# Hybrid GLA, pooling and gated DeltaNet layer on one core: decay sums moved into the projection stage, one decay matrix instead of two, merged forget-gate differences, keys moved by one place

## The chip, the cores and the metric

One core of a Trainium2 chip. The time is device microseconds (us) of one launch, which computes one layer for a prompt of 2048 tokens and a sample of 64 tokens.

## What is computed

Cut to what matters here:

```python
h = rmsnorm(x, norm_pre)
proj = h @ w_in                      # split: gla q,k,v,f,z; pool u,z; gdn q,k,v,a,b,z; three merge gates
# A: gated linear attention, chunked: logf = log_sigmoid(f @ wf2 + bf) / 16, b = cumsum(logf)
att = sum_d q[i,d] * k[j,d] * exp(b[i,d] - b[j,d])           # j <= i
# C: gated DeltaNet, chunked WY form: g = -exp(a_log) * softplus(a + dt_bias), beta = sigmoid(b)
G = cumsum(g)                                                # within a chunk
dec = exp(where(j <= i, G[i] - G[j], -inf))
m = beta[i] * (k @ k.T) * dec (j < i);   a_qk = (q @ k.T) * dec
u_bar, w = solve(I + m, [beta * v, beta * exp(G) * k])
q_dec = q * exp(G);   k_dec = k * exp(G_last - G);   state = exp(G_last) * state + k_dec.T @ u
# then head norms, SiLU gates, three branch projections, sigmoid merge gates, w_out, norm, residual
```

The kernel works in chunks of 128 tokens (16 for the prompt, numbered 0 to 15) and one of 64 (chunk 16, the sample).

## The kernel before

The program has five stages, each a block in which all engines run their own list of instructions and meet only at semaphores: the norm of x (norm_phase), the projections (project_phase), the chunks (chunk_phase), the branch projections and the output. All large products are made of three matmuls on operands split into a high and a low part (hi*hi, hi*lo, lo*hi).

**Projection stage.** TensorE multiplies one block of 128 columns of w_in after another (L411 to L413) with all 2112 tokens, in six tiles of 352. Each block's weights are split by GpSimd (L171, L173). The first block, F_SPECIAL, holds the rows from which decay g and beta come. VectorE works on these rows in a chain in which each link waits for the one before (L688 to L700): it ends with `X = X * nega * -1`, the decays g, on 4 partitions and 2112 tokens. Only then does VectorE take the tiles of the forget gates out of PSUM (L709), which TensorE makes in forget_gates (L428), waiting on side_free. SP stores the rows into scratch_feat, a DRAM tensor with 31 rows per partition and token; row R_GB has g and beta.

**Chunk stage.** Per chunk all engines work on the same chunk, and TensorE's list holds, between the chunk's own small matmuls, 48 steps of gate_products: a step is three matmuls 352 wide (L1255) of the merge-gate projection, whose last 16 blocks of columns were left for this stage. A tile of 352 tokens takes 8 steps, a chunk has 6 tiles. The steps stand in the list by hand, as filler where TensorE would wait. ScalarE copies each tile out (gates_out, L1456) when all its 8 steps are done and the row buffer is stored. The weights of a pair of chunks' gates, gate_w, are loaded by SP (L1129) and split by GpSimd into gate_w_hi and gate_w_lo (L1518, L1520), one block in the middle of a chunk and one at its end.

A wait is written now(engine, name, chunk) for something of this chunk and before(engine, name, chunk) for something that the previous chunk must have let go. The order of a chunk:

- SP loads the chunk's 31 rows (`inputs`, L1124, two buffers), two chunks ahead, after the stores of the outputs. Its sem_inc of h_good (L1171), after the first loads, lets the first gate product go.
- TensorE turns the row of g and beta (gbt, L1265), the values (vt, L1268) and the keys (kt, L1272). VectorE copies decay_beta (L1637). TensorE sums g down the chunk by a matmul with a triangle: as a column (g_col, L1277) and, with g broadcast as weights, as a row on all partitions (grow, L1282). ScalarE copies g_row (L1465) and makes e_row = exp(g_row) (L1469).
- GpSimd makes dec_qk = g_row - g_col and, with two additive masks, the arguments of two decay matrices (L1542 to L1549); ScalarE takes both exponentials (dec_kk L1474, dec_qk L1476). GpSimd makes k_dec (L1553), and q_dec (L1562) later.
- VectorE scans the forget gates (b_sum, L1633) and makes F: b_sum and 8 differences for each of two halves of 128 elements, 18 instructions (L1643 to L1652). ScalarE makes F its absolute value and then its exponential (L1480, L1483), with gates_out(c, 1) between them. VectorE multiplies keys by F (KF, L1691), GpSimd queries by F (QF, L1559).
- VectorE: d_col (L1659), k_tok (L1662), M from KK and dec_kk (L1667), M0, X, att from QK and dec_qk (L1679), XT, U (L1686), then KF.
- A triangular inverse in six more levels: for each level TensorE makes Z (L1370), turns XT (L1376), multiplies (L1385), and VectorE masks Z (L1704), copies X (L1708) and updates XT (L1717). The pairs of the linear attention (L1330) and the own pairs of level 1 (L1340) stand between them.
- U, outputs, state updates and head norms end the chunk.

## Time and profile before

| | us |
|---|---|
| median of 3 runs | 2978.51 (2978.11 to 2989.63) |
| span of the profiled execution | 2980.0 |
| TensorE matmul busy | 2742.3 (92%) |
| VectorE busy | 1141.0 (38%) |
| GpSimd busy | 840.4 (28%) |
| ScalarE busy | 664.2 (22%) |
| chunk stage, first to last gate product | 1211.1 to 2353.4 |
| mean granted TensorE clock, share of 2.4 GHz | 0.934 |

The profiled execution's own time is given only as its span. Busy times count an instruction from its start to its end, so one that waits for a resource counts as busy too, and a matmul's end is modelled and overlaps the next one's start. A span of an instruction group in the timeline runs from the first start to the last end.

### The profile page before, as it was taken

What the parts mean: (1) busy time and instruction counts of PE and PEld (TensorE: products, weight loads), DVE (VectorE), ACT (ScalarE), POOL (GpSimd) and SP (SyncE); (2) the same over time, 40 slices, a digit from 0 to 9 for tenths busy, and PEclk for the clock granted to TensorE, in tenths of its full rate; (3) what the DMA queues carried; (4) which work ended last, traced back from release to release, by engine and by line L of the source; (5) the groups of instructions that cost most, each with busy time, mean ns of one, the idle gap of its engine ahead of it and who ended that gap; (6) DMA issues with size and microseconds to landing.
All of it is one profiled execution on the core that took longest, in us unless ns stands there. A gap on an engine that the chain in (4) does not pass through costs nothing. (4 is left out here: it accounts for less than half of the span.)

```text
span 2980.0 us, 42847 instructions
## 1 busy us (share of the span) xinstructions
PE 2742.3 (92%) x17449; PEld 2602.6 (87%) x17449; DVE 1141.0 (38%) x1708; ACT 664.2 (22%) x997; POOL 840.4 (28%) x598
## 2 busy tenths in 40 slices
PE   6999999999999899799999989889999869999898
PEld 5899999999888899688888888888888759999786
DVE  5310112144656400444445444544545443331333
ACT  6121111112544111121221222112222132220221
POOL 1112111111111111344333444434444213442122
PEclk9999999999999999899999989989999769997799
DMA  4022411011111221322222243222221335542343
GB/s 159 23 108 94 174 65 58 29 51 57 44 65 66 72 74 44 114 64 64 64 67 64 64 141 110 79 77 74 71 67 38 114 123 169 170 157 76 114 144 107
DMA packets 208221, 261.80 MB, mean 88 GB/s; under 512 B 20864, under 2 KB 183056, under 8 KB 202320
## 3 DMA queue, kind: packets, MB, share of 16 engines
q1 hardware_dynamic: 201840, 251.01, 25.7%
q0 software_dynamic: 6240, 8.65, 1.0%
q8 instruction: 120, 1.97, 0.3%
q14 instruction: 21, 0.17, 0.0%
HBM read 160.34 MB, written 99.29 MB: 87 GB/s over the span
## 5 line engine op out<-in xcount | busy, mean ns | idle before, releaser
L411 PE MATMUL dense<-h_hi_first,w_hi 128*128 128x352 f32 x1080 | 356.0, 330 | 15.5 <-ACT row_y L658 8.5
L171 POOL TENSOR_TENSOR w_hi<-w_raw,zero 128x1024 fp32r<-128x1024 f32 x45 | 86.3, 1917 | 953.6 <-PE dense L413 916.0
L412 PE MATMUL dense<-h_lo_first,w_hi 128*128 128x352 f32 x1080 | 353.4, 327 | 0.0
L413 PE MATMUL dense<-h_hi_first,w_lo 128*128 128x352 f32 x1080 | 353.0, 327 | 0.0
L411 PE MATMUL dense<-h_hi_second,w_hi 128*128 128x352 f32 x1080 | 348.1, 322 | 0.0
L413 PE MATMUL dense<-h_hi_second,w_lo 128*128 128x352 f32 x1080 | 347.0, 321 | 0.0
L412 PE MATMUL dense<-h_lo_second,w_hi 128*128 128x352 f32 x1080 | 346.7, 321 | 0.0
L1255 PE MATMUL gate_bank<-h_hi_first,gate_w_hi 128*128 128x352 f32 x768 | 296.7, 386 | 33.0 <-SPq L1171 16.0
L1921 PE MATMUL y<-o_hi,wo_hi 128*128 128x256 f32 (+1 forms) x864 | 254.6, 295 | 26.3 <-DVE o_lo L1956 26.3
L1255 PE MATMUL gate_bank<-h_lo_first,gate_w_hi 128*128 128x352 f32 x768 | 260.5, 339 | 0.0
L1255 PE MATMUL gate_bank<-h_hi_first,gate_w_lo 128*128 128x352 f32 x768 | 259.2, 337 | 0.0
L1923 PE MATMUL y<-o_lo,wo_hi 128*128 128x256 f32 (+1 forms) x864 | 254.5, 295 | 0.0
L1925 PE MATMUL y<-o_hi,wo_lo 128*128 128x256 f32 (+1 forms) x864 | 254.5, 295 | 0.0
L411 PEld LDWEIGHTS dense<-h_hi_first,w_hi 128*128 128x128 f32 x1080 | 207.1, 192 | 19.3 <-ACT row_y L658 8.7
L412 PEld LDWEIGHTS dense<-h_lo_first,w_hi 128*128 128x128 f32 x1080 | 206.9, 192 | 1.1
L413 PEld LDWEIGHTS dense<-h_hi_first,w_lo 128*128 128x128 f32 x1080 | 206.9, 192 | 0.0
L413 PEld LDWEIGHTS dense<-h_hi_second,w_lo 128*128 128x128 f32 x1080 | 203.2, 188 | 0.0
L412 PEld LDWEIGHTS dense<-h_lo_second,w_hi 128*128 128x128 f32 x1080 | 202.9, 188 | 0.0
L411 PEld LDWEIGHTS dense<-h_hi_second,w_hi 128*128 128x128 f32 x1080 | 202.6, 188 | 0.0
L1921 PEld LDWEIGHTS y<-o_hi,wo_hi 128*128 128x128 f32 x864 | 177.8, 206 | 27.0 <-DVE o_lo L1956 27.0
L1255 PEld LDWEIGHTS gate_bank<-h_hi_first,gate_w_hi 128*128 128x128 f32 x768 | 157.3, 205 | 49.2 <-SPq L1171 16.3
L1577 POOL TENSOR_TENSOR gla_att<-gla_att,masked 128x256 f32<-128x256 f32 (+1 forms) x118 | 85.2, 722 | 334.2 <-DVE masked L1697 326.3
(227 smaller groups left out, 5288.3 us busy)
## 6 DMA issues: line engine op xcount, KB each, us to landing
inputs<-scratch_feat SPq DMA_DIRECT2D x16, 1984.0 KB, 8.9
scratch_feat<-row_y SPq DMA_DIRECT2D x28, 1056.0 KB, 4.9
gate<-scratch_gates SPq DMA_DIRECT2D x16, 1536.0 KB, 7.2
w_raw<-in_w_in SPq DMA_DIRECT2D x45, 512.0 KB, 5.4
scratch_gates<-gate_row SPq DMA_DIRECT2D x96, 176.0 KB, 1.8
gate_w<-in_w_in SPq DMA_DIRECT2D x32, 512.0 KB, 5.2
o_raw<-scratch_branch_out SPq DMA_DIRECT2D x8, 1536.0 KB, 10.4
scratch_gates<-row_y SPq DMA_DIRECT2D x8, 1056.0 KB, 5.0
```

The costliest lines, as they stand in the source:

```text
L171: nc.gpsimd.tensor_tensor(self.hi[:, p], raw, zeros, ALU.add).then_inc(self.high_ready, 1)
L411: nc.tensor.matmul(out, w_hi[:, p, k], h_hi[:, k, cols], start=(k == 0), stop=False)
L412: nc.tensor.matmul(out, w_hi[:, p, k], h_lo[:, k, cols], start=False, stop=False)
L413: mm = nc.tensor.matmul(out, w_lo[:, p, k], h_hi[:, k, cols], start=False, stop=(k == KD - 1))
L1255: mm = matmul(gate_bank[:, T % 2, 0:TW], w[:, r, k], h[:, k, t * TW:(t + 1) * TW], start=(k == 0 and part == 0), stop=(k == KD - 1 and par ...
L1577: ins = tt(own, own, halves_packed(masked[0:n, :, l, 0:n // 2], s), ALU.add)
L1921: nc.tensor.matmul(out, wo_hi[:, k, cols], o_hi[:, p, k, 0:n], start=(k == 4 * b), stop=False)
L1923: nc.tensor.matmul(out, wo_hi[:, k, cols], o_lo[:, p, k, 0:n], start=False, stop=False)
L1925: mm = nc.tensor.matmul(out, wo_lo[:, k, cols], o_hi[:, p, k, 0:n], start=False, stop=(k == 4 * b + 3))
```

## The change

Seven edits; all but the first are in the chunk stage.

1. In the projection stage VectorE writes the decays to T and then makes their sums within each chunk with 17 scans, 16 of 128 elements and one of 64, so that row R_GB of scratch_feat holds G instead of g.
2. SP loads, behind every load of inputs, the four rows of G onto all 128 partitions with one broadcasting DMA into g_row, which gets two buffers. The matmuls g_col and grow, their copies and the buffer g_col go. decay_beta now holds the column of G.
3. There is one decay matrix: ScalarE makes dec = |G_j - G_i| with four instructions, one per head, with the column as bias, and dec = exp(-dec). VectorE's M uses it as it is; GpSimd multiplies it by the triangle into att, and VectorE multiplies att by QK in place. GpSimd's three decay instructions go.
4. The scans of the forget gates write F directly, and each difference is one instruction for both halves.
5. keys() (the two KF instructions) moves from behind U to behind the diagonal of level 1, which is behind the first Z.
6. ScalarE instead of GpSimd makes gate_w_hi. TensorE's filler steps are spread anew, kt stands before vt, vtg before KK.
7. On TensorE, ScalarE and VectorE the last two chunks of the prompt stand outside the loop.

```diff
@@ project_phase, vector
-                link(nc.vector.tensor_scalar(X[g_rows, 0, 0:NT], X[g_rows, 0, 0:NT],
+                link(nc.vector.tensor_scalar(T[g_rows, 0:NT], X[g_rows, 0, 0:NT],
                                              small[g_rows, S_NEGA:S_NEGA + 1], -1.0, ALU.mult, ALU.mult))
+                for c in range(CHUNKS + 1):
+                    at = slice(c * P, c * P + (P if c < CHUNKS else NS_))
+                    last = nc.vector.tensor_tensor_scan(X[g_rows, 0, at], ones[g_rows, 0:at.stop - at.start],
+                                                        T[g_rows, at], 0.0, ALU.mult, ALU.add)
+                link(last)
@@ chunk_phase
+    FILL = {"start": 2, "turned": 5, "KK": 3, "QK": 7, "m0t": 3, "first": 4, "z": 3, "level": 2, "last": 2}
@@ sync, load
                     sp.dma_start(inputs[:, p, :, 0:n], feat[:, :, bass.ds(c * P, n)]).then_inc(in_landed[p], 16)
+                    g = feat[AT_G:AT_G + HEADS, R_GB, bass.ds(c * P, n)]
+                    sp.dma_start(g_row[:, p, :, 0:n], g.rearrange("(a h) t -> a h t", a=1)
+                                 .to_broadcast([P, HEADS, n])).then_inc(row_landed[p], 16)
@@ tensor, chunk
-                    gate_products(2)
+                    gate_products(FILL["start"])
...
                     transpose(ring[0][0:n, 0], I[:, R_GB, 0:n], ident).then_inc(S["gbt"], 1)
+                    before(pe, "dSg_taken", c)
+                    for h in range(HEADS):
+                        mm = transpose(ring[2][0:n, h], I[:, R_GDN_K + h, 0:n], ident)
+                    mm.then_inc(S["kt"], 1)
                     before(pe, "SSQg_taken", c)
                     for h in range(HEADS):
                         mm = transpose(ring[1][0:n, h], I[:, R_GDN_V + h, 0:n], ident)
                     mm.then_inc(S["vt"], 1)
...
-                    gate_products(2)
-                    now(pe, "gb_taken", c)
-                    matmul(ring[0][0:n, 1, 0:HEADS], upper[0:n, 0:n], decay_beta[0:n, 0, :],
-                           start=True, stop=True).then_inc(S["gcol"], 1)
-                    gate_products(5)
-                    now(pe, "gcol_taken", c)
-                    for h in range(HEADS):
-                        mm = matmul(ring[0][:, h, 0:n], decay_beta[0:n, 0, h:h + 1].to_broadcast([n, P]),
-                                    upper[0:n, 0:n], start=True, stop=True)
-                    mm.then_inc(S["grow"], 1)
+                    gate_products(FILL["turned"])
+                    now(pe, "gb_taken", c)
+                    for h in range(HEADS):
+                        mm = transpose(ring[0][0:n, h], I[:, R_GLA_V + h, 0:n], ident)
+                    mm.then_inc(S["vtg"], 1)
                     now(pe, "vt_taken", c)
                     for h in range(HEADS):
                         k = I[:, R_GDN_K + h, 0:n]
                         mm = matmul(ring[1][0:n, h, 0:n], k, k, start=True, stop=True)
                     mm.then_inc(S["KK"], 1)
-                    gate_products(5)
+                    gate_products(FILL["KK"])
                     now(pe, "kt_taken", c)
...
                     mm.then_inc(S["QK"], 1)
-                    gate_products(2)
-                    now(pe, "grow_taken", c)
-                    for h in range(HEADS):
-                        mm = transpose(ring[0][0:n, h], I[:, R_GLA_V + h, 0:n], ident)
-                    mm.then_inc(S["vtg"], 1)
-                    gate_products(6)
+                    gate_products(FILL["QK"])
...
                     mm.then_inc(S["m0t"], 1)
-                    gate_products(1)
+                    gate_products(FILL["m0t"])
...
-                        gate_products(3 if l == 1 else 2)
+                        gate_products(FILL["first"] if l == 1 else FILL["level"])
...
-                        gate_products({1: 1, LEVELS - 1: 2}.get(l, 0))
+                        gate_products({1: FILL["z"], LEVELS - 1: FILL["last"]}.get(l, 0))
@@ scalar, chunk
+                    act.wait_ge(row_landed[p], i * 16 + 16)
+                    activation(e_row[:, :, 0:n], g_row[:, p, :, 0:n], ACT.Exp).then_inc(S["e_row_ready"], 1)
+                    now(act, "gb_taken", c)
+                    for h in range(HEADS):
+                        last = activation(dec[0:n, h, 0:n], g_row[0:n, p, h, 0:n], ACT.Abs,
+                                          bias=decay_beta[0:n, 0, h:h + 1], scale=-1.0)
+                    last.then_inc(S["dec_diff"], 1)
+                    now(act, "dec_diff", c)
+                    activation(dec[0:n, :, 0:n], dec[0:n, :, 0:n], ACT.Exp, scale=-1.0).then_inc(S["dec_ready"], 1)
                     now(act, "vt", c)
                     copy(v_tok[0:n], ring[1][0:n]).then_inc(S["vt_taken"], 1)
-                    copy(g_row[:, :, 0:n], ring[0][:, :, 0:n]).then_inc(S["grow_taken"], 1)
...
-                    activation(dec_kk[0:n, :, 0:n], dec_kk[0:n, :, 0:n], ACT.Exp, scale=-1.0) \
-                        .then_inc(S["dec_kk_ready"], 1)
-                    activation(dec_qk[0:n, :, 0:n], dec_qk[0:n, :, 0:n], ACT.Exp) \
-                        .then_inc(S["dec_qk_ready"], 1)
...
                     gates_out(c, 2)
+                    split_gate_w(c, 0)
                     gates_out(c, 3)
...
                     head_norm(c, n, 1, "SSQg", "SSQg_taken", "rsg_ready")
+                    split_gate_w(c, 1)
+
+                def gate_w_to_high(c, r):
+                    act.wait_ge(gate_w_landed[r], c * 16 + 16)
+                    copy(gate_w_hi[:, r], gate_w[:, r]).then_inc(gate_w_high, 1)
+
+                def split_gate_w(c, r):
+                    if not (isinstance(c, int) and c >= CHUNKS - 1):
+                        gate_w_to_high(c + 1, r)
@@ gpsimd, chunk
-                    tt(dec_qk[0:n, :, 0:n], g_row[0:n, :, 0:n],
-                       g_col[0:n].rearrange("p (a b) -> p a b", b=1).to_broadcast([n, HEADS, n]),
-                       ALU.subtract).then_inc(S["diff_ready"], 1)
-                    now(pool, "diff_ready", c)
-                    before(pool, "KK_taken", c)
-                    tt(dec_kk[0:n, :, 0:n], dec_qk[0:n, :, 0:n], over_heads(masks[0:n, M_POS:M_POS + n]), ALU.add)
-                    tt(dec_qk[0:n, :, 0:n], dec_qk[0:n, :, 0:n], over_heads(masks[0:n, M_NEG:M_NEG + n]),
-                       ALU.add).then_inc(S["dec_args"], 1)
...
+                    now(pool, "dec_ready", c)
+                    tt(att[0:n, :, 0:n], dec[0:n, :, 0:n], over_heads(upper[0:n, 0:n]),
+                       ALU.mult).then_inc(S["dec_qk_ready"], 1)
@@ vector, chunk
                     for b in range(2):
-                        last = nc.vector.tensor_tensor_scan(b_sum[:, b, 0:n], ones[:, 0:n], I[:, R_LOGF + b, 0:n],
+                        last = nc.vector.tensor_tensor_scan(F[:, 0, b, 0:n], ones[:, 0:n], I[:, R_LOGF + b, 0:n],
                                                             0.0, ALU.mult, ALU.add)
...
+                    tt(d_col[0:n], g_row[0:n, p, :, n - 1], decay_beta[0:n, 0], ALU.subtract) \
+                        .then_inc(S["dcol_diff"], 1)
+                    bs = F[:, 0, :, 0:n]
+                    for l in range(LEVELS):
+                        blocks = bs.rearrange("p b (m t) -> p b m t", t=2 * s)
+                        tt(F[:, l + 1, :, 0:n].rearrange("p b (m t) -> p b m t", t=2 * s), blocks,
+                           blocks[:, :, :, s - 1:s].to_broadcast([P, 2, n // (2 * s), 2 * s]), ALU.subtract)
...
                             tt(gla_att[0:n, :, 0:n], ring[0][0:n, :, 0:n], over_heads(ident[0:n, 0:n]),
                                ALU.mult).then_inc(S["diag_taken"], 1)
+                            keys()
```

The other filler counts (3, 1, 1, 2, 2 at the end of a chunk) stay.

## Rows read from the trace of the kernel before

**Rows 1.** The head of the page.

```profile
span 2980.0 us, 42847 instructions
```

**Rows 2.** What TensorE waited for: line, releaser; us in total, times, longest.

```profile
PE ring L1282 <- DVE g_col L1655: 58.0, 16, 4.3
PE level_bank L1385 <- DVE Z L1704: 31.3, 16, 2.5
...
PE gate_bank L1255 <- SPq L1171: 16.0, 1, 16.0
...
PE ring L1315 <- DMA gla_state<-in_state_gla: 2.4, 1, 2.4
```

**Rows 3.** Stretches; after the engines' busy times: granted clock, DMA share, GB/s.

```profile
1291.40:1298.30 6.90, 5.96 (x25) 5.96 (x26) 1.74 (x8) 1.66 (x4) 3.11 (x3) 0.51 0.93 294
1311.90:1318.80 6.90, 5.99 (x26) 5.89 (x26) 2.30 (x5) 0.00 (x0) 4.64 (x2) 0.51 0.01 2
2078.20:2085.00 6.80, 3.52 (x27) 3.48 (x27) 3.99 (x19) 1.66 (x4) 1.63 (x3) 1.00 1.05 336
```

**Rows 4.** Timeline of TensorE in chunk 1: start, us, line, [idle before].

```profile
1283.29 0.27 PE L1265 MATMUL ring<-constants,inputs 128*128 128x128 f32 x1
...
1285.24 0.28 PE L1277 MATMUL ring<-decay_beta,masks 128*128 128x4 f32 x2
1285.38 0.41 PE L1255 MATMUL gate_bank<-h_hi_first,gate_w_hi 128*128 128x352 f32 x1
...
1287.71 0.32 PE L1255 MATMUL gate_bank<-h_hi_first,gate_w_lo 128*128 128x352 f32 x1
1292.34 2.07 PE L1282 MATMUL ring<-masks,decay_beta 128*128 128x128 f32 x8 [4.31 <-DVE g_col L1655]
...
1299.46 1.05 PE L1293 MATMUL ring<-inputs 128*128 128x128 f32 x8
...
1307.91 1.00 PE L1370 MATMUL level_bank<-XT,M 128*128 128x64 f32 x8
...
1310.24 0.43 PE L1255 MATMUL gate_bank<-h_hi_first,gate_w_hi 128*128 128x352 f32 x1
```

**Rows 5.** Timeline of VectorE in the same chunk.

```profile
1283.82 6.45 DVE L1650 TENSOR_TENSOR F<-b_sum 128x128 f32<-128x128 f32 x7
...
1290.52 1.49 DVE L1650 TENSOR_TENSOR F<-b_sum 128x128 f32<-128x128 f32 x7
...
1296.18 0.69 DVE L1662 TENSOR_TENSOR k_tok<-ring,d_col 128x512 f32<-128x512 f32 x1 [0.94 <-ACT d_col L1472]
...
1307.27 5.15 DVE L1691 TENSOR_TENSOR KF<-inputs,F 128x1024 f32<-128x1024 f32 x2
```

**Rows 6.** Timelines of ScalarE and GpSimd in the same chunk.

```profile
1283.24 0.63 ACT L1447 ACTIVATE sq_gla<-sq_gla 128x512 f32<-128x512 f32 x1
...
1283.94 1.30 POOL L1590 TENSOR_TENSOR out_gla<-out_gla,sq_gla 128x512 f32<-128x512 f32 x1 [0.54 <-ACT sq_gla L1447]
...
1287.23 2.48 POOL L1520 TENSOR_TENSOR gate_w_lo<-gate_w,gate_w_hi 128x1024 fp32r<-128x1024 f32 x1
...
1309.09 2.26 POOL L1562 TENSOR_TENSOR q_dec<-inputs,e_row 128x512 f32<-128x512 f32 x1
```

**Rows 7.** Groups by line, 1205 to 2365 us: busy us, mean ns | idle before.

```profile
L1480 ACT ACTIVATE F<-F 128x2304 f32<-128x2304 f32 (+1 forms) x17 | 35.0, 2057 | 0.0
...
L1469 ACT ACTIVATE e_row<-g_row 128x512 f32<-128x512 f32 (+1 forms) x17 | 10.5, 617 | 0.5
...
L1633 DVE TENSOR_TENSOR_SCAN b_sum<-constants,inputs 128x128 f32<-128x128 f32 (+1 forms) x34 | 12.3, 404 | 12.0 <-DMA inputs<-scratch_feat 11.5
```

**Rows 8.** Timeline of SP's DMA issues as the chunk stage begins.

```profile
1211.64 5.82 SPq L1129 DMA_DIRECT2D gate_w<-in_w_in  x1
```

**Rows 9.** Timelines of VectorE and GpSimd in the projection stage.

```profile
117.69 1.10 DVE L709 TENSOR_SCALAR row_t<-side,small 128x352 f32<-128x352 f32 x2 [4.71 <-PE side L428]
...
116.87 1.89 POOL L171 TENSOR_TENSOR w_hi<-w_raw,zero 128x1024 fp32r<-128x1024 f32 x1 [25.75 <-PE dense L413]
```

More of the change, by code:

```diff
@@ L1089, in chunk_phase @@
         in_landed = [held.add(nc.alloc_semaphore(f"in_landed{p}")) for p in range(2)]
+        row_landed = [held.add(nc.alloc_semaphore(f"row_landed{p}")) for p in range(2)]
         masks_landed = held.add(nc.alloc_semaphore("masks_landed"))
@@ L1506, in _ @@
                 preload(act, ACT_)
+                for r in range(2):
+                    gate_w_to_high(0, r)
                 act.sem_inc(gate_taken, 2)
@@ L1686, in chunk, with keys @@
                     tt(U[0:n], v_tok[0:n], ring[2][0:n], ALU.subtract).then_inc(S["R_taken"], 1)
[L1687 to L1692 removed]
+                    def keys():
+                        now(dve, "F_ready", c)
+                        before(dve, "kdtg", c)
+                        for b in range(2):
+                            k = I[:, R_GLA_K + b:R_GLA_K + b + 1, 0:n].to_broadcast([P, LEVELS + 1, n])
+                            last = tt(KF[:, :, b, 0:n], k, F[:, 1:LEVELS + 2, b, 0:n], ALU.mult)
+                        last.then_inc(S["KF_ready"], 1)
                     def take_pairs(h):
```

95 lines of the change are left out of this document (30 added, 65 removed).

## The prediction

> **What bounds the kernel now.** The first thing to read is the span [rows 1] and which stage the diff touches: the chunk stage, from 1211 to about 2408 us, plus a short piece of the projection stage. In the chunk stage TensorE is the engine that sets the pace, so the second view is the list of what TensorE waited for [rows 2]. Two waits stand out in it: before the decay-row matmuls of L1282, for VectorE's g_col (58.0 us over 16 chunks, 3.6 each), and before the first product of the levels, L1385, for VectorE's Z (31.3 us, 1.96 each).
>
> The third view is the table of stretches with the granted clock [rows 3]. Right after each of the two waits the clock stands at 0.51 for 6.9 us, which is the 1.2 GHz level; 2.4 GHz is 1.00. A stretch of 6.9 us at half the clock costs about 3.4 us, so the two waits cost nearly as much again in clock as in idle time. The last row is the exception: in one chunk the g_col wait of 3.28 us was followed by 2.4 GHz. I take from this that gaps of 2 to 4 us usually, but not always, cost a fall.
>
> The fourth view is the timeline of one chunk, engine by engine, in the order of the rows. For TensorE [rows 4] the gate products fill the gaps: 15 matmuls start between 1285.38 and 1287.71, 0.166 us apart, so a step of three is 0.5 us. For VectorE [rows 5] the same seven F differences take 6.45 us the first time and 1.49 us the second (0.21 each). GpSimd's rows [rows 6] say why: out_gla, gate_w_hi and gate_w_lo run from 1283.94 to 1289.7, exactly under the slow seven. VectorE gets about one difference through for each GpSimd instruction. The same is seen at the keys: the KF pair takes 5.15 us while q_dec, in between, takes 2.26 us instead of the 1.3 us of out_gla with as many elements; the extra 1.0 us is one KF. So a KF alone is about 1.05 us, and the two engines take strict turns when VectorE reads both operands from SBUF. k_tok, with one operand in PSUM, takes 0.69 us beside GpSimd's work and is not held.
>
> The Trainium skill says this more sharply (SBUF — State Buffer, Who interferes with whom): the port pair is an exclusive lock held for the whole instruction. By that rule moving keys() does not make it cheap; it only changes which GpSimd instruction it meets, and the trace agrees with the turns above.
>
> **The change, part by part.** I count from the start of the gbt transpose of a chunk (1283.29 in rows 4), in us.
>
> *Removed matmuls.* The eight row matmuls (L1282, rows 4) are 2.07 us busy at 1.2 GHz, so 1.0 at 2.4; the g_col product stands 0.14 us ahead of the next gate product (1285.24 to 1285.38), and one break in the gate products less saves about 0.1. That is 1.2 us per chunk. The 3.6 us wait for g_col goes too.
>
> *The new front.* Eight matmuls 128 wide, like QK's of 1299.46, are 1.05 us busy with their tail and keep TensorE 0.8 us from its next work; four turns take half of that. TensorE: gbt, kt, vt 0.9, five steps 2.5, four turns of gla_v 0.4: it stands before KK at 3.8 and needs v_tok. ScalarE is free at 0.6 (the last Exp of the previous chunk, rows 6) and must now do in order: the high half of gate_w, 1024 elements; e_row; four Abs; the Exp of dec; v_tok. From 512 elements in 0.617 us and 2304 in 2.06 [rows 7] an element costs 0.8 ns and a start 0.2 us: 1.0 + 0.6 + 4 x 0.3 + 0.6 + 0.6 = 4.0, done at 4.6. **New wait 1: 0.75 us** before KK. Its bounds are 0 (all instructions overlapping) and 1.3 (each Abs 0.14 dearer for its per-partition bias, which no row shows alone).
>
> By the Trainium skill (ScalarE: Activation LUTs, What ACT_TABLE_LOAD costs) an activation with a per-partition bias pointer takes 280 ns + 0.833 ns per element and neighbours overlap by 93 ns. An estimate from that page is 0.29 us for each Abs, so the sum would be the same to 0.1 us.
>
> *k_tok.* KK ends at 5.4, three steps bring TensorE to 6.9, where QK waits for k_tok. VectorE's 16 differences and two copies become eight differences of 256 elements, about 0.35 us each alone (0.21 for 128, 0.69 for 512, rows 5). GpSimd is busy under them: out_gla until 1.95, gate_w_lo 2.4 (rows 6; its high half has left for ScalarE, and three decay instructions are gone), k_dec 1.3, the new mask product 1.3, ending at 7.2 with VectorE's turns. Four differences go through in these turns, the other four after them: 8.7; k_tok 0.7: 9.4. **New wait 2: 2.5 us.** Bounds: 0 (if VectorE were not held, 8 x 0.35 would be done by 3.6) and 3.9 (one more turn behind a 1.3 us instruction). I take 2.5 because the seven slow differences of rows 5 follow the turns to 0.2 us.
>
> *The middle.* QK until 10.2, seven steps and m0t 3.9, three steps 1.5, R 0.8, four steps 2.0: Z of level 1 starts at 18.4. Z and the own pairs are 2.33 (1307.91 to 1310.24): 20.7. VectorE does gla_att (0.65) and only then the keys, at 21.4. Z's mask is no longer behind them, so the 1.96 us wait before L1385 goes. But L1717's update of XT, which level 2 waits for, is now behind the keys. TensorE has three steps, the products and two steps, 3.4 us, and is at level 2 at 24.1.
> GpSimd meanwhile: ScalarE's F Exp waits behind gates_out(1), whose tile is complete 16 steps into the chunk, at 13.2; 0.4 + 2.1 gives F_ready at 15.7; QF, twice gate_w_lo's 1024 elements, 4.7, q_dec 1.3: 21.7; then gate_w_lo, whose high half is ready. So KF runs 21.7 to 22.8, gate_w_lo takes its turn to 25.2, the second KF is done at 26.3, the update at 26.7. **New wait 3: 2.6 us** before level 2. Bounds: 0.1 (no turn lost) and 3.9 (q_dec and gate_w_lo both before a KF).
>
> *Sum per chunk.* Off: 1.2 + 3.6 + 1.96 = 6.8. On: 0.75 + 2.5 + 2.6 = 5.85. Net 1.0 us less, 16 us in 16 chunks.
>
> *Clock.* Wait 3 is longer than the Z wait it replaces and is followed by short matmuls, so I keep its low stretch in every chunk. Wait 2 is shorter than g_col's usual 3.4 to 4.3; with the exception of rows 3 in mind I let the clock fall in two chunks of three. Saved: 5.3 x 3.4 = 18 us. The ends are 0 and 54.
>
> *Once.* (a) SP now issues a row load behind each inputs load, before it raises h_good, on which TensorE's first gate product waits (L1171 in rows 2). The issue that follows an inputs load took 5.82 us [rows 8]. The second row load will take that place: +6 us, bounds 1 and 8. In the loop the same block falls where SP blocks on gate_w now, some 10 us ahead of the first ScalarE instruction that needs that gate_w: nothing there, and if this cover went, gates_out(3), U and the head norms would queue on ScalarE behind that wait. The rows have a whole chunk to land. (b) The 17 scans on VectorE. The first side tile was taken at 117.69, after 4.71 us of idle, so the chain ended at 112.98 [rows 9]. A scan of 128 elements is 0.40 us busy [rows 7], about 0.34 with its overlap, so the chain is 5.8 us longer, and GpSimd's weight split at 116.87 holds the last ones, so the side tile is taken near 122.7: +5 us (bounds 1, and 8.5 with a clock fall). (c) The sample chunk gains nothing: its R waits for the state to land (2.4 us in rows 2). *At nothing:* att now first holds the masked decay, with the same two engines and waits as before it; peeling the last two chunks leaves their work unchanged, covered by TensorE's queued gate products; without that cover, a few us.
>
> **Total.** -16 - 18 + 11 = -23 us on a span of 2980.0. The page gives only the span, which stands 1.5 above the median of 2978.51. Forecast 2956.
>
> **The rivals.** A measurement here can tell 0.5%, 15 us, from no change.
> 1. *The clock falls at both new waits in all chunks*, as it did at the g_col gap of rows 3. Then -16 + 11 = -5: 2974, no change. For: the gaps before L1385, 2.0 us on average, were followed by one too. Chance 0.25.
> 2. *Level 2 becomes the bound (slower).* If both KF instructions meet a GpSimd instruction that has not begun when they ask (q_dec, then gate_w_lo), wait 3 is 3.9 and the low clock that follows covers Z, x_turned, pairs and the next level, 1.7 us more per chunk. With rival 1's clock that is -5 + 16 x (1.3 + 1.7) = +43; with wait 3 grown alone about +16. It decides from 2.2 us over my per-chunk sum. For: q_dec and the keys come within 0.3 us of each other. Against: the first KF asked while q_dec ran, in my schedule. Time 2995 to 3021, chance 0.17.
> 3. *The differences miss GpSimd*, because ScalarE hands over gate_w's high half later than out_gla ends, or k_dec waits for e_row. Then wait 2 is under 1 us and the clock stays up there: 1.7 + 2.3 more per chunk, -23 - 64: 2891. Chance 0.10.
> 4. *The keys miss gate_w_lo.* Wait 3 is 0.2, and its low stretch goes: -23 - 16 x 5.8: 2863. Against: the high half is ready 2 us before q_dec ends. Chance 0.08.
> My forecast, 2920 to 2963, has 0.40. That the change does not do what it says I rule out: nothing issues the removed matmuls any more.
>
> **The numbers.** Faster by over 0.5%: 0.40 + 0.10 + 0.08 = 0.58; within: 0.25; slower: 0.17. The likeliest case alone spans 2920 to 2963; the range that leaves out 2 in 10 is 2880 to 2995.
>
> **What would show it.** In the profile after, TensorE's waits should list KK behind ScalarE's v_tok (about 12 us), QK behind VectorE's k_tok (about 40), and L1370 behind XT's update (about 42); g_col and Z must be gone. One or two low stretches per chunk, on average 1.7. The difference instructions should show some over 1.5 us and others at 0.35; gate_w_lo should have every second one near 3.4 us. The forecast is wrong if k_tok's wait is under 1 us, or if level 2 has none, or if TensorE's first gate product is not late by about 6 us.

## The result and the profile after

The changed kernel takes 3008.9 us (median of 17 runs, 2989.6 to 3023.9) against 2981.6 for the kernel before (17 runs on the same chip). The ratio is 1.0085, with a 95% interval of 1.0067 to 1.0103: slower by 0.85%. The forecast was 2956, faster. One execution of a later kernel, the one with the early start, ran at a mean clock of 0.553 and took 4415 us; it is left out of that kernel's ratio, and its median without it is 2854.55.

The profiled execution spans 3022.2 us, 42.2 more than [rows 1]; it is the slowest of the 17, and the medians lie 27 us apart. This is the page's head and its table of busy times:

```profile
span 3022.2 us, 42253 instructions
PE 2773.5 (92%) x17279; PEld 2629.2 (87%) x17279; DVE 1123.5 (37%) x1538; ACT 697.2 (23%) x1063; POOL 737.4 (24%) x531
```

TensorE issues 170 matmuls fewer and is busy 31 us longer, which points at the clock. The mean granted clock fell from 0.934 to 0.916. As the clock has two levels here, 1.00 and 0.50, the time at the low one is 2 x (1 - mean) x span: 393 us before, 508 after. I use this sum for the profiled execution of every run below and call it the low time. It varies within one kernel, and the time goes with it: over the 17 runs of the changed kernel it runs from 430 us, in the one of 2989.6, to 508, in the one of 3023.9, with 469 at the median. That is about 0.44 us of time for each microsecond more at the low level.

What TensorE waited for in the chunk stage (us in total, times, longest), to be read against [rows 2]:

```profile
PE level_bank L1350 <- DVE XT L1692: 39.3, 20, 2.4
PE ring L1278 <- DVE k_tok L1635: 34.2, 16, 2.6
PE gate_bank L1245 <- SPq L1159: 25.7, 1, 25.7
PE gate_bank L1245 <- SPq L1176: 13.3, 1, 13.3
...
PE ring L1295 <- DMA gla_state<-in_state_gla: 7.5, 1, 7.5
...
PE ring L1273 <- ACT v_tok L1455: 3.5, 5, 1.8
```

L1350 is Z's product of level 2 and up, L1278 is QK, L1273 KK, L1245 the gate products, L1295 R. The waits for g_col and Z, 89.3 us together, are gone. The three new ones are where they were forecast, 77.0 us together. The one before level 2 is 2.43 us in 15 of the 16 chunks; the last has no gate_w left to split. So the waits inside the chunks fell by 12 us, and yet the kernel is slower.

Where the time is lost shows in one chunk of the second half. This is TensorE's timeline of chunk 12, only the rows with an idle time ahead and the products of the levels:

```profile
2116.27 1.25 PE L1278 MATMUL ring<-inputs 128*128 128x128 f32 x8 [2.11 <-DVE k_tok L1635]
...
2135.20 1.97 PE L1350 MATMUL level_bank<-XT,M 128*128 128x64 f32 x8 [2.43 <-DVE XT L1692]
...
2144.76 1.80 PE L1350 MATMUL level_bank<-XT,M 128*128 128x64 f32 x8
...
2154.15 1.29 PE L1350 MATMUL level_bank<-XT,M 128*128 128x64 f32 x8
2159.48 1.00 PE L1350 MATMUL level_bank<-XT,M 128*128 128x64 f32 x8
2164.51 1.00 PE L1350 MATMUL level_bank<-XT,M 128*128 128x64 f32 x8
```

From level 4 to 5 and from 5 to 6 it is 5.33 and 5.03 us, but from level 2 to 3 and from 3 to 4 it is 9.56 and 9.39. The table of stretches (start and end; length, the engines' busy times, then the granted clock, DMA share, GB/s) gives the reason:

```profile
2117.20:2120.60 3.40, 3.40 (x15) 3.40 (x14) 2.03 (x4) 0.57 (x1) 0.00 (x0) 0.50 1.00 236
2120.60:2134.20 13.60, 12.11 (x83) 11.42 (x81) 6.67 (x6) 4.35 (x5) 9.26 (x4) 1.00 0.31 108
2134.20:2154.60 20.40, 19.40 (x83) 18.51 (x84) 5.26 (x10) 0.45 (x1) 0.00 (x0) 0.50 0.00 1
2154.60:2180.00 25.40, 25.21 (x193) 23.96 (x193) 11.35 (x24) 3.47 (x7) 5.13 (x7) 1.00 0.04 15
```

After the wait for k_tok the clock is at the 1.2 GHz level for 3.4 us, half of what it was after the g_col wait [rows 3]. In this chunk it then falls 1.0 us before the wait ahead of level 2 ends, and stays low for 20.4 us, three times the 6.9 of [rows 3]; 19.4 of them count as busy. Chunks 9 to 14 all look like this one.

The first half is mixed. Chunk 5 has the same wait of 2.43 us and the same work behind it, but the clock falls 1.6 us after the wait has ended, and comes back after 6.8 us:

```profile
1613.94 1.11 PE L1350 MATMUL level_bank<-XT,M 128*128 128x64 f32 x8 [2.43 <-DVE XT L1692]
```

```profile
1615.60:1622.40 6.80, 6.80 (x30) 6.68 (x31) 1.67 (x3) 0.00 (x0) 0.00 (x0) 0.51 0.01 2
```

Over the 15 chunks with this wait the stretch is 6.8 us in four, 10.2 in one, 17 in two, 20.4 in seven and 27.2 in one, 16 on average. In the seven with 20.4 the clock fell 0.8 to 1.0 us before the wait ended. After the wait for k_tok there is a stretch of 3.4 us in 11 chunks and none in the other five.

The instructions that make TensorE wait are as forecast. VectorE's and GpSimd's timelines of chunk 12, first at its head, then at the keys:

```profile
2108.41 2.35 DVE L1619 TENSOR_TENSOR d_col<-g_row,decay_beta 128x4 f32<-128x4 f32 x1
2110.68 4.60 DVE L1629 TENSOR_TENSOR F<-F 128x256 f32<-128x256 f32 x7
...
2129.93 4.88 DVE L1665 TENSOR_TENSOR KF<-inputs,F 128x1024 f32<-128x1024 f32 x2
2134.73 0.41 DVE L1692 TENSOR_TENSOR XT<-XT,level_bank 128x256 f32<-128x256 f32 x1
```

```profile
2108.35 2.39 POOL L1511 TENSOR_TENSOR gate_w_lo<-gate_w,gate_w_hi 128x1024 fp32r<-128x1024 f32 x1
2110.70 1.53 POOL L1532 TENSOR_TENSOR k_dec<-inputs,e_row 128x512 f32<-128x512 f32 x1
...
2129.13 1.28 POOL L1544 TENSOR_TENSOR q_dec<-inputs,e_row 128x512 f32<-128x512 f32 x1
2130.37 3.35 POOL L1511 TENSOR_TENSOR gate_w_lo<-gate_w,gate_w_hi 128x1024 fp32r<-128x1024 f32 x1
```

Even a d_col of four elements takes 2.35 us, until the gate_w_lo that began 0.06 us earlier lets it through. At the keys the first KF waits for the end of q_dec, gate_w_lo comes in between, and the second KF is done at 2134.7.

The start of the stage, SP's DMA issues, against [rows 8]:

```profile
1207.44 0.34 SPq L1152 DMA_DIRECT2D masks<-in_masks  x1
...
1208.99 7.63 SPq L1111 DMA_DIRECT2D g_row<-scratch_feat  x1
...
1218.11 9.11 SPq L1111 DMA_DIRECT2D g_row<-scratch_feat  x1
```

The first gate product starts at 1227.32 instead of 1211.12. The masks' load was issued at 1201.00 before and at 1207.44 now, so 6.4 us come from the projection stage and 9.8 from SP's queue.

My theory after this view: the wait before level 2 lets the clock fall, and it does not come back while TensorE does the thin work of the first levels (few gate products between small matmuls that wait for one another); all the rest of the change gains. The rivals were that the new spread of the gate steps starves the levels whatever VectorE does, and that the loss lies in the projection stage and the start.

### The profile page after: what moved, and what is told of

The parts are those of the page before. It is cut to its first block and busy times, and to the rows that moved or that the text cites. A ratio compares the mean times of both kernels' runs of the same rounds, so it can differ in the third digit from the quotient of the medians.

```text
span 3022.2 us, 42253 instructions
## 1 busy us (share of the span) xinstructions
PE 2773.5 (92%) x17279; PEld 2629.2 (87%) x17279; DVE 1123.5 (37%) x1538; ACT 697.2 (23%) x1063; POOL 737.4 (24%) x531
## 5 line engine op out<-in xcount | busy, mean ns | idle before, releaser
L1245 PE MATMUL gate_bank<-h_hi_first,gate_w_hi 128*128 128x352 f32 x768 | 297.4, 387 | 47.5 <-SPq L1159 25.7
L1245 PE MATMUL gate_bank<-h_lo_first,gate_w_hi 128*128 128x352 f32 x768 | 264.1, 344 | 0.0
L1245 PE MATMUL gate_bank<-h_hi_first,gate_w_lo 128*128 128x352 f32 x768 | 263.6, 343 | 0.0
L392 PEld LDWEIGHTS dense<-h_hi_first,w_hi 128*128 128x128 f32 x1080 | 206.6, 191 | 19.5 <-ACT row_y L639 8.7
L1245 PEld LDWEIGHTS gate_bank<-h_hi_first,gate_w_hi 128*128 128x128 f32 x768 | 159.1, 207 | 63.5 <-SPq L1159 26.0
```

The lines of the kernel that those rows point to most:

```text
L392: nc.tensor.matmul(out, w_hi[:, p, k], h_hi[:, k, cols], start=(k == 0), stop=False)
L1245: mm = matmul(gate_bank[:, T % 2, 0:TW], w[:, r, k], h[:, k, t * TW:(t + 1) * TW], start=(k == 0 and part == 0), stop=(k == KD - 1 and par ...
```

## The experiments

Twelve kernels ran, three or five rounds each. "Before" is 2982 to 2983 us in all of them.

### Keys put back

The keys() call goes from behind the diagonal back to behind U; everything else of the change stays.

```diff
+                    keys()
...
-                            keys()
```

> The changed kernel with one part undone: keys() stands behind U again, so VectorE's update of XT is no longer behind the keys, and the mask of Z is. Theory 1 (the wait of TensorE before level 2, and the low clock that then lasts through the levels, is what made the change slow): the wait before the Z product of level 2 (39.3 us in the changed kernel) is gone, a wait before the xt product of level 1 comes instead, about 0.9 us per chunk, 15 in all (1.96 before, less two more gate steps); the stretches of 20 us at the low clock are gone, so that the low time is near the 397 us of the kernel before instead of 508. Time: 3009 - 24 for the waits - about 50 for the clock, near 2935. Theory 2 (the new spread of the gate steps leaves the levels with too little work, whatever VectorE does): the long low stretches stay, and only the 24 us of waits go: near 2985. Theory 3 (the cost lies in the projection stage and in the first row load alone): no more than the wait's difference either, 2985.

Measured: 2889.95 us, ratio 0.9687 (0.9671 to 0.9702). What TensorE waited for in this kernel:

```profile
PE ring L1278 <- DVE k_tok L1635: 34.4, 16, 2.7
...
PE level_bank L1365 <- DVE Z L1679: 11.4, 16, 0.7
```

The wait before level 2 is gone, the 0.7 us wait before level 1's product came as expected, and no long stretch follows it; the stretch from before level 1's product through the levels of a chunk is at full clock:

```profile
2031.80:2060.00 28.20, 27.48 (x215) 26.24 (x214) 13.27 (x24) 0.82 (x2) 9.85 (x10) 1.00 0.02 7
```

The mean clock is 0.953, the low time 272 us instead of 508. One edit of seven accounts for 119 us; the other six together make the kernel before 93 us faster. The two rivals, which gave 2985, are out. My own theory gave 2935, because it left the low time at 397 us, that of the kernel before. There the g_col wait and the Z wait were each followed by 6.8 us in most chunks; here only the k_tok wait is followed by a low stretch, 3.4 us in 10 of the 16 chunks. That is as in the changed kernel (11), so what went is the stretch at the levels.

### GpSimd's gate_w_lo behind the keys, then behind the differences too

```diff
+                        now(pool, "KF_ready", c)
                         split_gate_w(c + 1, 0)
```

> The changed kernel with one wait added: GpSimd does not begin gate_w_lo of the middle of the chunk before VectorE has finished the keys. Nothing else differs. Theory 1: the keys take about 1.1 us each instead of 1.1 and 3.4 to 4.9, XT comes in time, the wait before level 2 falls from 2.4 to at most 0.3 us per chunk, and with it the long low stretch: -35 us of waits and 50 to 90 us of clock, 2885 to 2925. Theory 2 (the spread of the gate steps): -35 us only, about 2975, with the long low stretches still there. Rival 3 (the low clock comes from the wait before QK, whatever follows): the low stretch behind QK stays and now runs through to the levels, 2975 too.

Measured: 2877.25 us, ratio 0.9650 (0.9634 to 0.9665), just below the range given. The keys stay where the change put them. The wait for k_tok is unchanged (34.7 us in 16) and the long stretches at the levels are gone all the same, so the rival that put them down to it is out. Only GpSimd waits, and TensorE's wait before level 2 is 0.25 us in this chunk:

```profile
2020.90 1.11 PE L1350 MATMUL level_bank<-XT,M 128*128 128x64 f32 x8 [0.25 <-DVE XT L1693]
```

```diff
+                    if swap:
+                        load_h(2)
                     if not (isinstance(c, int) and c >= CHUNKS - 1):
+                        now(pool, "F_diffs", c + 1)
                         split_gate_w(c + 1, 1)
-                    if swap:
-                        load_h(2)
```

> As the run before it, and GpSimd's gate_w_lo at the start of a chunk also waits, until VectorE's eight differences of that chunk are done. So VectorE has no GpSimd instruction beside its differences but out_gla. Expected by the account of turns: the differences take about 0.35 us each but for two, k_tok is ready 2 us earlier, and the wait before QK (34.2 us in the changed kernel) falls to under 10; with it the low stretch of 3.4 to 6.8 us behind it in most chunks: 25 us of waits and about 25 of clock less than the run before, 2840 to 2880. If VectorE's differences are slow for another reason than GpSimd's SBUF traffic, the wait before QK stays at 2 us and the time is that of the run before. What it may cost: k_dec now stands behind gate_w_lo that starts later, so the outputs and state updates of the chunk could wait for k_dec; by the schedule it has 40 us to spare.

Measured: 2860.25 us, ratio 0.9596 (0.9568 to 0.9624), in the range. The wait for k_tok fell from 34.2 to 7.7 us in total, 0.5 at most, and k_dec's delay cost nothing that TensorE's waits show. The median came down by 17 us where 25 us of waits and some clock had been promised: the wait at the change of halves (L1176) had grown to 19.7 us. That is taken up below.

### The kernel before with its keys moved

The same move alone, in the kernel before.

> The kernel before with that one part of the change alone: keys() moved to behind the diagonal of level 1. The Z wait (31.3 us) goes, and a wait before the Z product of level 2 comes. TensorE has only one gate step behind Z here where the changed kernel has three, and GpSimd does both halves of gate_w there, so the new wait is about 1 us longer than in the changed kernel, 3.5 us per chunk, 56 us. Theory 1: it is followed by the long low stretch through the levels; 2981 - 31 + 56 + 20 to 60 for the clock: 3025 to 3065. Theory 2 (it was the spread of gate steps): the stretch of 6.8 us behind the wait stays as it was, near 3005. If moving the keys is harmless here, 2981 or below.

Measured: 3040.93 us, ratio 1.0199 (1.0177 to 1.0222), in the range of theory 1.

```profile
PE ring L1282 <- DVE g_col L1655: 57.9, 16, 4.3
PE level_bank L1370 <- DVE XT L1719: 54.1, 20, 4.7
```

The Z wait of [rows 2] (31.3 us) went, 54.1 us came, and the mean clock fell to 0.923, 468 us of low time. The move is harmful by itself, without anything else of the change (58 us here, 119 in the changed kernel).

### Gate steps moved around the wait

First, two steps go from ahead of the wait to behind level 2's first products.

```diff
-    FILL = {..., "z": 3, "level": 2, "last": 2}
+    FILL = {..., "z": 1, "level": 2, "last": 2, "behind": 2}
...
+                        if l == 2:
+                            gate_products(FILL["behind"])
```

> The changed kernel with two gate steps of the middle of each chunk (1 us) moved from ahead of the wait before level 2 to behind its products, ahead of the pairs. The idle time there grows from 2.4 to about 3.4 us per chunk, and the work that follows it is denser. Theory 1a (the long low stretch comes from the idle time alone): it stays 20 us in as many chunks or comes in more of them, and the time rises by 16 us for the waits and up to 30 for the clock, to 3025 to 3055. Theory 1b (it comes from idle time followed by the thin matmuls of the levels): the clock falls as often, but comes back earlier, low stretches of 7 to 10 us instead of 20, 3009 + 16 - 40 to 60, 2965 to 2985.

Measured: 2990.88 us, ratio 1.0032 (1.0018 to 1.0046). The wait rose to 54.2 us in 20, as meant, and the low time fell from 508 to about 413 us (mean clock 0.931; over all runs the median went from 469 to 412). The kernel was 18 us faster with 15 us more of waiting. Neither theory had the number, but the direction is that of 1b: with two more gate steps behind the wait the stretches were 6.8 to 13.7 us long and 3.4 once, never 17 to 27. The longest, in chunk 1, with the clock falling 1.2 us before the wait's end:

```profile
1322.40:1336.20 13.80, 12.54 (x53) 12.04 (x53) 3.37 (x6) 0.00 (x0) 0.00 (x0) 0.51 0.00 1
```

The fair comparison is between chunks in which the clock falls at the same point of the wait, 0.8 to 1.2 us before its end. With the levels at once behind it the stretch is 20.4 to 20.6 us in all 17 such chunks (seven of the changed kernel, five with one step moved, two with two keys more, three of the kernel before with its keys moved). With two gate steps behind it, it is 13.6 to 13.8 us in all four. At the Z wait of the kernel before, where the fall came 0.6 to 1.7 us before the end, it is 6.8 to 7.0 in all 14. So the work behind the wait does set the stretch once the moment of the fall is the same. Where the clock falls after the wait's end, the stretch before the levels is 6.8 to 17 us, and 27.2 once; what decides there, and what sets the moment of the fall, no run here shows.

Then two steps, and in a later run one, go from ahead of the first Z to behind it.

```diff
-    FILL = {..., "first": 4, "z": 3, ...}
+    FILL = {..., "first": 2, "z": 5, ...}
```

> The changed kernel with two gate steps moved from ahead of the first Z to behind it, still ahead of the wait before level 2, so that this wait falls from 2.4 to about 1.4 us if the keys end when they did (they are asked for 1 us earlier, but GpSimd's turns fix their end). Nothing is taken away from GpSimd or VectorE. If the fall of the clock hangs on the length of the wait, the long low stretches go in most chunks: -16 us for the waits and -50 to -90 for the clock, 2900 to 2945. If any wait at this place makes it fall, they stay, and the time is about 2993.

> The changed kernel with one gate step, not two, moved from ahead of the first Z to behind it: the keys are asked for 0.5 us earlier instead of 1.0. By the account of turns q_dec has then still begun 0.3 us before the keys ask, so the first key instruction waits for q_dec's end as it did, the second for gate_w_lo, both end when they did, and the wait before level 2 stays 2.4 us: 3009, no change. If the time went with the moment of asking in a smooth way, it would be half way between 3009 and 2877, 2943.

Measured: 2877.46 us for two steps, ratio 0.9656 (0.9633 to 0.9678); 3013.76 for one, 1.0093 (1.0069 to 1.0117). One step of 0.5 us changes nothing, two give 131 us. VectorE's and GpSimd's timelines of chunk 1 with two steps:

```profile
1312.83 3.52 DVE L1665 TENSOR_TENSOR KF<-inputs,F 128x1024 f32<-128x1024 f32 x2
1316.27 0.41 DVE L1692 TENSOR_TENSOR XT<-XT,level_bank 128x256 f32<-128x256 f32 x1
```

```profile
1312.98 2.28 POOL L1544 TENSOR_TENSOR q_dec<-inputs,e_row 128x512 f32<-128x512 f32 x1
1315.22 3.34 POOL L1511 TENSOR_TENSOR gate_w_lo<-gate_w,gate_w_hi 128x1024 fp32r<-128x1024 f32 x1
```

In the first of the two runs my expectation was wrong in its mechanism: I expected the keys to end when they did, and a wait of 1.4 us. But the keys now ask 0.15 us before q_dec begins. So the first KF runs ahead of q_dec (which is held and takes 2.28 us), the second ahead of gate_w_lo, the pair takes 3.52 instead of 4.88 us, and TensorE has no wait at level 2 at all (2.6 us in 4 places are left of 39.3 in 20). For one step I then worked by the turns, and that held: q_dec has still begun first, and the wait is 38.9 us in 20, against 39.3. The moment of asking counts only by which side of a GpSimd instruction's start it falls on. The Trainium skill's rule of the exclusive lock (SBUF — State Buffer, Who interferes with whom) agrees with these rows.

### A wait of chosen length at level 2

In the kernel where gate_w_lo waits for the keys, VectorE does its second key instruction twice, or three times (`m` is 1 or 2), so that TensorE waits though GpSimd has no part in it.

```diff
+                        for j in range(m):
+                            last.then_inc(again, 1)
+                            dve.wait_ge(again, c * m + (j + 1))
+                            last = tt(KF[:, :, 1, 0:n], k, F[:, 1:LEVELS + 2, 1, 0:n], ALU.mult)
                         last.then_inc(S["KF_ready"], 1)
```

> The kernel in which gate_w_lo waits for the keys (2877 us, no wait before level 2), with VectorE's second key instruction done twice, one behind the other: nothing meets it on GpSimd, so the update of XT comes about 1.1 us later and TensorE waits about 1 us before level 2. This is a wait of chosen length at the place in question, with the turns taken out of it. If the clock's fall depends on the length of the wait, 1 us is short enough (0.7 us before the products of level 1 brought none when the keys were put back): +16 us for the waits alone, 2893. If any wait there makes the clock fall through the levels, + 16 + 16 x up to 8 for the clock, 2950 or more.

> The same with the second key instruction done three times: XT comes about 2.2 us later, a wait of 2.1 to 2.4 us before level 2 as in the changed kernel, though GpSimd has no part in it. If idle time there and the thin work behind it are the whole cause of the long low stretch, the low time of the chunks comes back to near the 399 us of the changed kernel and the time to 2877 + 35 + 70 to 100: 2980 to 3010. If GpSimd's and VectorE's contention matters for TensorE's clock in some other way, only the waits come: 2912.

Measured: 2967.23 us for one, ratio 0.9943 (0.9924 to 0.9963); 3019.73 for two, 1.0151 (1.0117 to 1.0184). Against 2877 that is 90 and 142 us, of which the waits are 21 and 41 (27.4 and 48.3 us against 6.8). The second is 10 us above the range given. TensorE in one chunk of the run with one more, and its stretches:

```profile
2026.50 1.10 PE L1351 MATMUL level_bank<-XT,M 128*128 128x64 f32 x8 [1.50 <-DVE XT L1698]
2034.05 1.80 PE L1351 MATMUL level_bank<-XT,M 128*128 128x64 f32 x8
2043.44 1.80 PE L1351 MATMUL level_bank<-XT,M 128*128 128x64 f32 x8
```

```profile
2028.40:2045.40 17.00, 17.00 (x77) 16.43 (x76) 3.70 (x8) 0.45 (x1) 0.23 (x1) 0.51 0.03 12
```

And in the run with two more:

```profile
2055.10:2075.50 20.40, 18.98 (x81) 18.08 (x82) 5.70 (x10) 0.45 (x1) 2.35 (x1) 0.51 0.00 1
```

The second run shows what was in question: idle time at this place, with the thin work behind it, costs the clock without GpSimd. The low time is 458 us (477 at the median of its four runs, against 469), the kernel 11 us slower than the changed one with a wait of 2.76 instead of 2.43 us. In the first run I was wrong. I had thought that about a microsecond would do no harm, as 0.7 us before level 1's product does none; the wait came out at 1.5 us, and the clock fell behind it in all 16 chunks, 0.3 to 3.3 us after its end. Its low time is 416 us.

The chunks shown are the longest cases. With one more key the stretch is 6.8 us in ten chunks, 10.2 in three, 13.6 in two and 17 in the one above, where the fall comes 2.3 us after the wait's end. With two more it is 6.8 in seven, 10.2 in four, 17 in three and 20.4 in two.

Nor is a long wait needed. The three kernels with both waits of gate_w_lo idle 0.25 us before level 2, and in four of their 48 chunks the clock fell all the same, about 3 us later, for 13.6 us in which TensorE was busy throughout. This is one of them, from the first of the three:

```profile
2119.00:2132.60 13.60, 13.60 (x60) 13.08 (x60) 3.21 (x6) 0.45 (x1) 0.00 (x0) 0.51 0.00 1
```

### SP's queue

The three raises of h_good go ahead of both row loads at the start, and then, in one more kernel, ahead of chunk 9's loads at the change of halves. Both have the two waits of gate_w_lo.

```diff
-                load(0, 0)
+                load(0, 0, row=False)
                 load_gate_w(0, 1, 0)
-                load(1, 1)
-
                 for t in range(3):
                     sp.sem_inc(h_good[t], CHUNKS // 2)
+                load_row(0, 0)
+                load(1, 1)
```

> The kernel with both waits of gate_w_lo (2860 us), and with SP's three raises of h_good at the start of the stage ahead of both row loads, with the first inputs and the gate weights before them. TensorE's first gate product then waits for the gate weights and their split alone: the wait of 25.7 us becomes 10 or less, and the low stretch of 27 us behind it may shrink. If the row loads cost what I now put down to them (7.7 and 9.0 us of issue on SP, of which 9.7 delay the start) and the rest of the wait is SP's other issues, 2860 - 10 to 20: 2840 to 2850. If the start is bound by the landing of the gate weights, no more than 5 us come.

> The kernel with the early start and both waits of gate_w_lo (2855 us), and at the change of halves SP raises h_good ahead of chunk 9's loads of inputs and row instead of behind them. In that kernel the row load's issue there took 15 us and TensorE waited 19.5 us, with 20 us at the low clock behind it. If the row load on SP's queue is the cause, that wait falls to under 5 us: -15 for it and about -8 for the clock, 2830. If the landing of the second half of h is the cause, nothing changes: 2855.

Measured: 2854.88 us, ratio 0.9570 (0.9552 to 0.9588), and 2832.56, ratio 0.9512 (0.9486 to 0.9538). The first can hardly be told from the 2860 without it: the wait at the start fell from 25.7 only to 20.3 us. SP's issues show a part of the reason:

```profile
1211.01 0.64 SPq L1109 DMA_DIRECT2D inputs<-scratch_feat  x1
1211.70 7.56 SPq L1121 DMA_DIRECT2D gate_w<-in_w_in  x1
```

Now the gate weights' load stands behind the inputs load and takes the 7.6 us that the row load took. It is the place behind an inputs load that costs, not the row load as such. SP raises h_good at about 1219.3, though, and TensorE starts at 1224.59, released by ScalarE (L1505), which signals behind its second gate_w_hi; that one starts at 1224.43, when the second gate weights have landed. So the landing of the gate weights now bounds the start, the case for which I had expected at most 5 us. At the change of halves the second kernel's wait fell from 19.5 to 3.8 us, as expected. The issue of the row load there, from SP's timeline of the kernel with the two waits of gate_w_lo:

```profile
1714.86 15.06 SPq L1111 DMA_DIRECT2D g_row<-scratch_feat  x1
```

The same row of SP's timeline in the best kernel:

```profile
1722.71 4.83 SPq L1115 DMA_DIRECT2D g_row<-scratch_feat  x1
```

And its row in the list of TensorE's waits:

```profile
PE gate_bank L1250 <- SPq L1180: 3.8, 1, 3.8
```

This kernel, 2832.6 us, is 5% faster than the one before and the best of all; its six runs lie at 2827 to 2834 (four) and 2848 (two).

### The two waits in the kernel before

Nothing of the change, but GpSimd's splits wait for the keys and for the differences, as above.

> The kernel before with nothing of the change but with the two waits on GpSimd: its split of gate_w (both halves here) in the middle of the chunk waits for the keys of the chunk, the one at the end waits for the eighteen difference instructions of the next chunk. If the turns of GpSimd and VectorE at SBUF are what set the g_col wait (58 us) and the Z wait (31 us), both fall to under 10 us and the low stretches behind them mostly go: 2981 - 80 for the waits - 40 for the clock, near 2860. Against it: the split of 4.6 us now stands right ahead of GpSimd's three decay instructions, so M could come late and TensorE wait before m0t or R; then 2900 to 2950. If it is no better than 2981, the turns are not the cause in this kernel.

Measured: 2947.31 us, ratio 0.9898 (0.9869 to 0.9928): not 2860, but within the 2900 to 2950 given for a late M. M was not the main reason, though.

```profile
PE level_bank L1385 <- DVE Z L1706: 49.8, 16, 3.3
...
PE ring L1305 <- DVE M L1674: 13.4, 13, 1.1
PE ring L1282 <- DVE g_col L1657: 6.7, 6, 2.5
```

The g_col wait went from 58.0 to 6.7 us, so there the turns with GpSimd were the cause. M was late by 13.4 us in all, as feared. The Z wait grew from 31.3 to 49.8 instead of falling. I had looked only at gate_w's split. GpSimd's and VectorE's rows of one chunk show what the keys met instead:

```profile
1925.06 5.66 POOL L1559 TENSOR_TENSOR QF<-inputs,F 128x1024 f32<-128x1024 f32 x2 [4.38 <-ACT F L1483]
```

```profile
1925.22 6.58 DVE L1693 TENSOR_TENSOR KF<-inputs,F 128x1024 f32<-128x1024 f32 x2
```

QF begins 0.16 us ahead of the keys (2.86 in [rows 5]'s chunk), so each KF waits for a whole QF, and the pair takes 6.58 us instead of 5.15. What can be said is that the remedy gives 35 us in the kernel before and 149 in the changed one: the change is worth having once its levels don't wait.

## Why the prediction was wrong

The sum without the clock held. The projection's scans and what follows them delayed the stage by 6.4 us (I said 5); in the other kernels with this projection stage it is 5 to 9. Its mechanism held as well: 15 of the 17 scans take 0.39 us or less, the two beside GpSimd's weight split 2.0 and 2.5, and the first side tile is taken at 122.58, for which I had 122.7. The start of the stage was 9.8 us late on SP's queue (6). The waits inside the chunks: KK for v_tok 0.43 us in 4 of the 16 chunks and 1.8 in the sample's (0.75 in all 16; ScalarE's four Abs took 1.26 us in chunk 1, as summed), QK for k_tok 2.1 (2.5), level 2 for XT 2.43 in 15 (2.6). The g_col and Z waits went entirely. ScalarE, GpSimd's turns and the order KF, gate_w_lo, KF were as written. Take 12.3 us of waits and the forecast 19 of removed matmuls off, add 6.4 + 9.8, and two small items that I did not have, 4.6 at the change of halves and 5.1 for the sample's state that lands later against TensorE (7.5 instead of 2.4): the balance is 5 us less than before. My own sum without clock was 16 - 11 = 5 us less.

**The step that failed is the clock term.** It read: "Wait 3 is longer than the Z wait it replaces and is followed by short matmuls, so I keep its low stretch in every chunk", that is 6.9 us of low clock, and 18 us saved in all through wait 2. Wait 2 did what was asked of it and more: a low stretch in 11 of 16 chunks, the two in three assumed, of 3.4 us and not 6.9. Behind the g_col wait the clock was low for 89 us in the kernel before, behind wait 2 for 38 in the changed one. But wait 3's stretch is 16 us on average, 6.8 at best, 20.4 in seven chunks and 27.2 in one: behind the Z wait the clock was low for 99 us in the kernel before, behind wait 3 for 242 in the changed one. The low time rose by 115 us where it was to fall by 36, and the span by 42 us; with the rest at -5, the clock cost some 47 us, 0.4 us for each microsecond at the low level. Between the medians it is 27 us of time for some 75 of low time. The error was to take the length of a low stretch from a place (before L1385) where it ended by itself in [rows 3], though the argument named what differed: behind the Z wait stand one product, two gate steps and then the levels; behind wait 3 stand the levels at once. The run with steps moved behind the wait shows that this matters: 13.7 us instead of 20.4 where the clock falls at the same point. It is not all that matters, since the same wait before the same work gave 6.8 to 27.2 us.

Rival 2 had the place, the sign and the mechanism ("the low clock that follows covers Z, x_turned, pairs and the next level"). But it made it depend on a wait of 3.9 us and priced it at 1.7 us per chunk. The wait was 2.43 and the net price of the clock about 2.9 (47 / 16). Its condition did not arise, so that its range, 2995 to 3021, holds the measured 3008.9 is in part luck. Rival 1 (the clock falls at both places in all chunks) counted too many falls, 32 where there were 26, and gave 2974, because it too had 6.9 us for each. Rival 4 (the keys miss gate_w_lo) did not come true in the changed kernel, but in the run with two steps moved, which took 2877 us; I had written 2863.

A second, smaller omission: of SP's queue I costed the start and the loop, and not the change of halves, where h_good stands behind chunk 9's loads. It was 4.6 us in the changed kernel, and 15.7 (19.5 less 3.8) in a faster one.

Not settled: what sets the moment at which the clock falls, and with it most of the spread between 6.8 and 27.2 us; and how short a wait at level 2 does no harm: behind 0.25 us the clock fell in 4 of 48 chunks, behind 1.5 in all 16, and nothing in between was tried.

## What to carry to other kernels

Before a wait is moved, read what stands behind it: 2 to 2.5 us of idle time cost 3.4 us at the low clock or none ahead of dense matmuls, and 6.8 to 27 ahead of thin, dependent ones, so an unavoidable wait belongs ahead of the densest work. When VectorE and GpSimd both work in SBUF, plan their order by an explicit wait on the engine that has time (one added line gave 132 us here), since without it half a microsecond in an unrelated place decides which goes first. On a DMA queue, count the slot behind a many-row load as the expensive one, and put signals ahead of it.

## What was not expected of the hardware

- TensorE stayed at 1.2 GHz through 20.4 us of the levels' work though 19.4 of them count as busy; with two gate steps behind the wait no stretch was over 13.8 us. The same wait before the same work gave 6.8 us in other chunks.
- A wait of 1.5 us was followed by a fall in all 16 chunks, 0.3 to 3.3 us after its end. With 0.25 us of idle time, 4 of 48 chunks had a fall of 13.6 us.
- One kernel's 17 runs spread over 34 us, and their order is nearly that of their low time, 430 to 508 us.
- A VectorE instruction on 4 elements took 2.35 us, the full time of the GpSimd instruction that had begun 0.06 us ahead of it.
- The issue of a DMA behind an inputs load at the start of the stage took 5.8 to 9.1 us, whichever DMA it was (7.6 for gate weights and for a row alike), and a row load at the change of halves 4.8 to 15.1.
